# Two of six weight pieces per expert issued by ScalarE in place of SyncE, and the order of TensorE's work on expert 30, in a streamed 32-expert layer

## The reference

```python
def moe_ffn(h, w_router, b_router, w1, b1, w2, b2):
    logits = (t @ w_router + b_router)
    top_val, top_idx = lax.top_k(logits, TOP_K)          # TOP_K = 4 of 32
    gate = jax.nn.softmax(top_val, axis=-1)
    ...
    def expert_block(args):
        xb, e = args
        hid = xb @ w1[e] + b1[e]                         # w1[e]: 1024 x 2048, 8 MB
        glu, lin = jnp.split(hid, 2, axis=-1)
        glu = jnp.minimum(glu, SWIGLU_LIMIT)
        lin = jnp.clip(lin, -SWIGLU_LIMIT, SWIGLU_LIMIT)
        act = glu * jax.nn.sigmoid(SWIGLU_ALPHA * glu) * (lin + 1)
        return act @ w2[e] + b2[e]                       # w2[e]: 1024 x 1024, 4 MB
    ...
    out = jax.ops.segment_sum(ys * buf_gate[:, None], buf_tok, num_segments=n)
```

## Time and profile before

| | |
|---|---|
| median of 3 runs | 1232.0 us (1230.29 to 1233.63) |
| profiled execution, time | 1232.9 us |
| profiled execution, span from first to last instruction | 1231.1 us |
| TensorE busy | 1170.0 us, 95% |
| VectorE, ScalarE busy | 396.7 us (32%), 224.4 us (18%) |
| DMA read from HBM | 457.87 MB, 373 GB/s over the span |
| pieces of 2 MB issued by SyncE | 129 + 42 + 21 = 192 |
| wring, blk, vz pieces, issue to landing (median) | 35.6, 35.1, 35.7 us |
| granted TensorE clock, mean | 0.994 |

### The profile page before, as it was taken

How to read it: one execution, slowest core, us unless ns; L and a number is a source line. 1 busy time by engine, 2 the same in 40 slices (tenths; PEclk the granted TensorE clock), 3 DMA queues, 4 the chain that set the end, 5 groups by cost and what they waited for, 6 DMA issues and landing times.

```text
span 1231.1 us, 14120 instructions
## 1 busy us (share of the span) xinstructions
PE 1170.0 (95%) x5773; PEld 586.2 (48%) x5773; DVE 396.7 (32%) x716; ACT 224.4 (18%) x338; POOL 45.1 (4%) x32
## 2 busy tenths in 40 slices
PE   9999999999999999999998989899999999899897
PEld 8988888884343443434332323334333333233336
DVE  2679944643121221222121222212121212221127
ACT  4766564350000000000000000000000000000017
POOL 6600000010000000000000000000000000000000
PEclk9999999999999999999999999999999999999899
DMA  8655488789999999999999999999999999999980
GB/s 272 201 170 205 137 296 326 275 303 400 427 431 426 426 429 426 431 427 428 430 428 427 427 432 426 429 429 425 428 430 426 428 428 428 426 429 429 425 331 35
DMA packets 62382, 459.60 MB, mean 373 GB/s; under 512 B 7385, under 2 KB 16993, under 8 KB 37506
## 3 DMA queue, kind: packets, MB, share of 16 engines
q1 hardware_dynamic: 62338, 458.95, 90.7%
HBM read 457.87 MB, written 1.06 MB: 373 GB/s over the span
## 4 chain that ended last, share of the span: by engine, by line
PE 69%; DMA 24%; DVE 4%; ACT 2%; issue 1%; ACTq 0%; SPq 0%; DVEq 0%
PE bank L1028 23%; PE bank L1066 14%; DMA wring<-in_w_dram 12%; DMA vz<-in_w_dram 12%; PE bank L710 5%; PE bank L712 5%; PE bank L711 5%; PE bank L991 4%; PE bank L1000 2%; PE bank L1034 2%; PE bank L1057 1%; PE bank L775 1%; PE bank L785 1%; PE bank L780 1%; PE bank L697 1%
## 5 line engine op out<-in xcount | busy, mean ns | idle before, releaser
L1028 PE MATMUL bank<-wring,hT 128*64 128x512 f32 x1360 | 312.4, 603 | 17.0 <-DMA wring<-in_w_dram 13.4
L1028 PEld LDWEIGHTS bank<-wring,hT 128*64 128x64 f32 x1360 | 94.7, 138 | 201.3 <-issue 172.7
L1066 PE MATMUL bank<-wring,xbcT 128*64 128x512 f32 x672 | 150.7, 595 | 7.3 <-DVE xbcT L1998 6.3
L1979 DVE TENSOR_SCALAR xbcT<-bank 128x512 f32<-128x512 f32 x32 | 22.2, 693 | 412.7 <-PE bank L1034 412.7
L1488 ACT ACTIVATE xbcT<-xbcT 128x512 f32<-128x512 f32 x32 | 20.2, 631 | 495.2 <-DVE xbcT L1979 495.2
L2000 DVE COPY xbcT<-bank 128x256 f32<-128x256 f32 x32 | 13.6, 425 | 253.5 <-PE bank L1007 253.5
L1066 PEld LDWEIGHTS bank<-wring,xbcT 128*64 128x64 f32 x672 | 46.5, 137 | 101.4 <-issue 91.9
L1626 DVE TENSOR_TENSOR blk_lo<-blk,blk_hi 128x2048 fp32r<-128x2048 f32 x32 | 73.1, 2288 | 39.8 <-ACT blk_hi L1303 39.8
L1028 PE MATMUL bank<-vz,hT 128*64 128x512 f32 x336 | 78.9, 600 | 5.5 <-DMA vz<-in_w_dram 5.5
L1493 ACT ACTIVATE xbcT<-bank 128x512 f32<-128x512 f32 x31 | 18.5, 597 | 352.3 <-PE bank L1066 352.3
L1028 PE MATMUL bank<-blk,hT 128*64 128x512 f32 x352 | 79.7, 594 | 1.8 <-DMA blk<-in_w_dram 1.8
(11 more groups left out here) (300 smaller groups left out, 1213.6 us busy)
## 6 DMA issues: line engine op xcount, KB each, us to landing
wring<-in_w_dram SPq DMA_DIRECT2D x129, 2048.0 KB, 35.6
blk<-in_w_dram SPq DMA_DIRECT2D x42, 2048.0 KB, 35.1
vz<-in_w_dram SPq DMA_DIRECT2D x21, 2048.0 KB, 35.7
blk<-in_w_in_dram SPq DMA_DIRECT2D x28, 1024.0 KB, 5.2
blk<-in_w_branch_a_dram SPq DMA_DIRECT2D x4, 1024.0 KB, 5.5
blk<-in_w_branch_b_dram SPq DMA_DIRECT2D x4, 1024.0 KB, 7.2
blk<-in_w_out_dram SPq DMA_DIRECT2D x4, 1024.0 KB, 5.2
x<-in_x_dram SPq DMA_DIRECT2D x4, 512.0 KB, 5.3
```

Of the source, the lines that this page charges most:

```text
L1028: last = mm(bank[dh * SLOTS:(dh + 1) * SLOTS, :], xgT[:, k, :], at(c)[:, kk * 2 * F + off + dh * W:kk * 2 * F + off + (dh + 1) * W], start ...
L1066: last = mm(YB[dh * SLOTS:(dh + 1) * SLOTS, :], units[:, kk * P + c * SLOTS:kk * P + (c + 1) * SLOTS], at(W1C + c)[:, kk * D + dh * W:kk * ...
L1979: ts(g_sb, GLU[:, :], LIMIT, None, ALU.min).then_inc(g_done, 1)
```

## The change

`ACT_LOADS = (1, 2)`: from expert 2 on, pieces 1 and 2 of an expert's six are issued by ScalarE, both behind its `take_y` of the expert two before; in the list of the last twelve these are positions 1 and 2 of each six: (30, 1), (30, 2), (31, 3) and (30, 4). SyncE issues the other four, with the waits that it had. The gate weights of the embedding wait on SyncE until the last but one of the 192 pieces has landed.

On TensorE, an odd expert's gate rows are transposed into GLU ahead of `turned_units`, in place of into TB behind `rows_out`; an even expert first waits until VectorE has copied them. Expert 30 takes its four w1 pieces one after another, then gathers for expert 31, turns its units, and scatters expert 29's rows.

```diff
+ACT_LOADS = (1, 2)
@@ SyncE, in the loop
                     for c in range(NCH):
-                        g = NCH * (2 + r) + c
-                        slot = g % NSLOT
-                        sp.wait_ge(chunk_used, NCH * GROUP * i + (g - NSLOT + 1))
-                        sp.dma_start(slots[slot], chunk_src(GROUP * i + (2 + r), c)).then_inc(loaded[slot], 16)
+                        if c not in ACT_LOADS:
+                            g = NCH * (2 + r) + c
+                            slot = g % NSLOT
+                            sp.wait_ge(chunk_used, NCH * GROUP * i + (g - NSLOT + 1))
+                            sp.dma_start(slots[slot], chunk_src(GROUP * i + (2 + r), c)).then_inc(loaded[slot], 16)
@@ SyncE, after the loop
+            last_but_one = NCH * E - 2
             sp.wait_ge(chunk_used, NCH * E - NSLOT + 1)
+            sp.wait_ge(loaded[last_but_one % NSLOT], 16 * (last_but_one // NSLOT + 1))
             load_gate(0, 0)
@@ TensorE, units_of
+                if side == 0 and not alone:
+                    pe.wait_ge(selT_done, j)
@@ TensorE, expert
                 if side:
+                    pe.wait_ge(g_done, j + 1)
+                    selected(GLU)
                     turned_units(j)
...
                 rows_out(actT, at, arrived)
-                selected(TB)
+                if side == 0:
+                    selected(TB)
@@ TensorE, last_two
-                units_of(first, *stream(first), 0, between=rows_between)
+                units_of(first, *stream(first), 0)
+                gather(last_chosen)
+                pe.wait_ge(selT_done, first)
                 turned_units(first)
+                scatter(lambda: None)
@@ ScalarE
+            def freed_by_rows(j, r):
+                for c in ACT_LOADS:
+                    g = NCH * (r + 2) + c
+                    act.dma_start(slots[g % NSLOT], chunk_src(j + 2, c)).then_inc(loaded[g % NSLOT], 16)
+            with act.Fori(0, LOOPED // GROUP) as i:
+                for r in range(GROUP):
+                    gated(GROUP * i + r)
+                    take_y(GROUP * i + r)
+                    freed_by_rows(GROUP * i + r, r)
```

More of the change, by code:

```diff
@@ L490, in bcast, with chunk_src @@
             return ap.to_broadcast(shape)
+        def chunk_src(e, c):
+            if c < W1C:
+                r = c * RW1 * P
+                return w1[0, e, r:r + RW1 * P, :].rearrange("(p k) n -> p (k n)", k=RW1)
+            r = (c - W1C) * RW2 * P
+            return w2[0, e, r:r + RW2 * P, :].rearrange("(p k) n -> p (k n)", k=RW2)
         block = ctx.enter_context(nc.Block())
@@ L537, in _ @@
             load(ln_b, vec(sgu_ln_b), ln_loaded)
[L539 to L545, removed]
             def load_chunk(g):
@@ L610, in _ @@
                     for c in range(NCH):
-                        g = NCH * (2 + r) + c
-                        slot = g % NSLOT
-                        sp.wait_ge(chunk_used, NCH * GROUP * i + (g - NSLOT + 1))
-                        sp.dma_start(slots[slot], chunk_src(GROUP * i + (2 + r), c)).then_inc(loaded[slot], 16)
-            for g in range(NCH * (E - GROUP), NCH * E):
[L617 to L621, removed]
+                        if c not in ACT_LOADS:
[3 more added lines that the diff above has]
+                            sp.dma_start(slots[slot], chunk_src(GROUP * i + (2 + r), c)).then_inc(loaded[slot], 16)
+            for g in range(NCH * (E - GROUP), NCH * E):
+                if g % NCH not in ACT_LOADS:
+                    sp.wait_ge(chunk_used, g - NSLOT + 1)
+                    e, c = (g // NCH, g % NCH) if g < NCH * (E - 2) else LAST_TWO[g - NCH * (E - 2)]
+                    load(slots[g % NSLOT], chunk_src(e, c), loaded[g % NSLOT])
+            last_but_one = NCH * E - 2
             sp.wait_ge(chunk_used, NCH * E - NSLOT + 1)
+            sp.wait_ge(loaded[last_but_one % NSLOT], 16 * (last_but_one // NSLOT + 1))
             load_gate(0, 0)
@@ L1129, in stream, with last_chosen @@
                     return at, arrived
[L1131 to L1138, removed]
-                units_of(first, *stream(first), 0, between=rows_between)
+                def last_chosen():
+                    pe.wait_ge(sel_done, first + 2)
+                    pe.wait_ge(y_copied, first)
+                units_of(first, *stream(first), 0)
+                gather(last_chosen)
+                pe.wait_ge(selT_done, first)
                 turned_units(first)
+                scatter(lambda: None)
                 pe.wait_ge(actT_done, first + 1)
@@ L1501, in gate_high @@
                     fn(pg_hi[b][:, k * W:(k + 1) * W], gate_raw(b, k), ACT.Copy, scale=gain).then_inc(pg_high, 1)
[L1503 to L1506, removed]
+            def freed_by_rows(j, r):
[7 more added lines that the diff above has]
+                    freed_by_rows(GROUP * i + r, r)
+            for j in range(LOOPED, E - 2):
                 gated(j)
@@ L1512, in _ @@
                 take_y(j)
+                if j < E - 4:
+                    freed_by_rows(j, j)
+                else:
+                    for c in ACT_LOADS:
+                        g = NCH * (j + 2) + c
+                        e, piece = LAST_TWO[g - NCH * (E - 2)]
+                        act.dma_start(slots[g % NSLOT], chunk_src(e, piece)).then_inc(loaded[g % NSLOT], 16)
             gated(E - 2)
@@ L1966, in _, with expert @@
             cp(n_extra[:], cnt[:, 0:1]).then_inc(extra_done, 1)
-            def expert(j, ahead=0, last_one=False):
+            def expert(j, ahead=0, odd=False, last_one=False):
                 if ahead:
@@ L1999, in expert @@
                 dve.wait_ge(selT_filled, j + 1)
-                cp(selgT.rearrange("p t s -> p (t s)"), (GLU if last_one else TB)[:, 0:TT * P]).then_inc(selT_done, 1)
+                cp(selgT.rearrange("p t s -> p (t s)"), (GLU if odd or last_one else TB)[:, 0:TT * P]).then_inc(selT_done, 1)
             with dve.Fori(0, E // 2 - 1) as i:
                 expert(2 * i, ahead=2)
-                expert(2 * i + 1)
+                expert(2 * i + 1, odd=True)
             expert(E - 2, ahead=1)
```

## The result

The changed kernel takes 1238.58 us (median of 7 runs, 1236.13 to 1239.49) against 1232.0 for the kernel before (7 runs); the ratio is 1.0048, interval 1.0037 to 1.0060. It is **slower**, by 4.6 to 7.4 us. Its profiled execution took 1238.6 us, with a span 5.7 us over that of the earlier trace rows.

What follows compares the result with a forecast made beforehand. DMA was taken to bound the kernel up to the 30th expert, at 4.89 us a piece, then TensorE. +11.3 (3 dry, 9.8 order, less 1.5 slack) - 5.8 = +5.5 us gave 1237.5, range 1226 to 1252.

Steps and rivals of the forecast that it cites:

- the hole: At expert 0's rows, about 303 to 306 us: DMA engines run dry until ScalarE issues; +3 us (2 to 4).
- Part 1: ScalarE's later issue of pieces 1 and 2: free in steady state, +3 us once, at the first expert.
- Part 2: Second ring takes turns, ScalarE's pieces pass SyncE's queue; at the end piece 180 begins 11.3 us later, dry time included.
- In mid-kernel this only moves TensorE's waits: Before the end, the changed landing order costs nothing, as DMA stays busy.
- The list of waits: TensorE would wait before the first and fourth pieces of an expert, and not before the second and third.
- Part 3: TensorE's work from the start of piece 180 to the last rows out: 48.3 us in place of 54.1, -5.8.
- the clock's 2.1: Around expert 31's start: 2.1 us gained because the granted clock would not fall, with the gather filling the 2.58 us idle.
- The rest is small: Early selT_done wait, odd experts' earlier transposes and later gate weights: no cost; gate weights covered by 9 us.
- A: Rival, no passing: ScalarE's DMAs share the ring or are served by age; -0.7, 1231.3 us; chance 13%.
- B: Rival, two rings carry more: 433 GB/s against 428, -10 us, 1227.5 with part 1; chance 17%.
- C: Rival, taking turns costs: 0.45 us a packet adds 430 us, once a piece +54 (1291), or nothing; chance 15%.

Runs made afterwards that it cites:

- the small edits undone: Changed kernel without the gate weights' wait and the early wait for selT_done, odd experts' gate rows in TB behind rows out: 1238.66 us, ratio 1.0052.

## Why the prediction was right

It said 1237.5; 1238.6 was measured. The case that it forecast is the one that came, and its steps can be set beside the trace:

| step | predicted | measured |
|---|---|---|
| data flow again after the hole | 306.7 | 307.5 |
| transfers lost | 3 | 2.9 |
| pieces to come when 180 lands | 9 | 9.0 |
| 180 begun | 1145.5 | 1145.80 |
| expert 31 begun | 1167.2 | 1166.94 |
| wait for its third piece | 0.7 | 1.06 |
| clock, 1160 to 1170 | 1.00 | 1.00 |
| last rows out begun | 1193.8 | 1193.91 |
| span | +5.5 | +5.7 |

The close match is in part luck. Piece 12 landed at 305.38 before and at 306.24 after, ahead of everything that the change moves: 0.9 of the 5.7 us between the spans, and of the moments in the table, is the chance of these two executions (over all kernels here that piece landed from 304.0 to 307.9). And by the medians the loads cost 11.1 us, where the prediction had 11.3, but the new order gave back 4.5, where it had 5.8; so the measured +6.6 is 1.1 above the +5.5.

**Part 1** held in size. ScalarE issues its first DMA 0.16 us after its copy starts, not 0.5, and in this execution the copy stood 1.07 us later than in the earlier trace rows; the first packet follows its issue by 1.04 us, as the prediction took it. The end of the hole is therefore 0.8 us later than predicted, but the pieces ahead of it are too (piece 12 by 0.9 us), so its length stays.

**Part 2** was the step with the least under it, one packet of another kind at 810, and it held. (The trace of before has 19 such packets of q8 between 320 and 1170, not one.) When both queues have pieces, each queue's land 9.79 us apart: in the changed kernel 181 at 1129.76 and 182 at 1139.54, 178 at 1133.34 between them. By the Trainium skill (DMA: Bandwidth & Descriptors, "Queues, rings and completion order") a DMA engine goes round the queues that have work, a packet at a time; these landings agree with even turns that are shorter than a piece (whole pieces in turn would land 4.89 us apart, not 3.6 and 6.2), but don't show that a turn is one packet. What was wrong is the sentence "In mid-kernel this only moves TensorE's waits". It is true of the time of the transfers, but it drew the line at expert 30. Passing at expert 29 costs too, when nothing later covers it: 1.8 to 1.9 us by the traces, in a difference of 2.4 by the medians; in the changed kernel the larger passing behind it does. The list of waits was too short as well: besides those before first and fourth pieces there are some before pieces 4 and 5, up to 3.1 us. By engine line and releaser (us in total, times, longest):

```profile
PE bank L1033 <- DMA wring<-in_w_dram: 13.4, 12, 1.3
...
PE bank L1071 <- DMA wring<-in_w_dram: 8.4, 6, 1.8
...
PE bank L1071 <- DMA blk<-in_w_dram: 6.8, 3, 3.1
```

**Part 3** came out at -6.0 (48.1 in place of 54.1) for -5.8, but not all of that is the order. With the same loads and TensorE's old order the stretch takes 52.7 us, so the new order is worth 4.6 in the traces (4.5 by the medians). The other 1.4 us come from the clock of the execution before: it was low for longer there, so that expert 30's turn and expert 31's first piece took 1.11 and 5.75 us, against 0.66 and 4.87 (granted 0.50 from 1158 to 1164 before; 0.64 and 0.51 from 1170 to 1174 in the other). The term that the prediction sized too high is thus the clock's 2.1. The same order on the old loads gives only 4.3, since there TensorE waits for the pieces that it no longer spaces out with other work. That the clock wouldn't fall was right. The reason given, that the idle time of 2.58 us is filled, isn't enough: in the kernel whose gather was moved by half there are only 0.85 and 0.79 us idle, and the clock is still at 0.50 behind them.

**The rest is small** held: no difference with the small edits undone.

**The rivals.** A, no passing, falls with the issue-to-landing times of the two queues (19.2 and 37.8 us). B, a higher rate, and C, a cost at each turn, fall together with 427 GB/s at a share of 1.01 from 1000 to 1150. Between 320 and 1170 a 16 KB packet of q1 took 0.615 us and one of q10 0.616; in the kernel with q1 alone, 0.615. C's 0.45 us belongs to the packets of q8, which do take 1.07 us in the mean with one data queue and with two, and not to the turn. B's 433 GB/s was ten microseconds of a rate that scatters about 428. The Trainium skill says (same page, "Issuing engines are not separate DMA queues") that more issuers save only issuing time; on the rate the trace agrees (427 with two, 428 with one).

The sum, from the one-queue kernel up: -4.3 for TensorE's order, +7.1 for the passing in the last two experts, +2.1 to 4.3 for the hole (+3.0 by the landings): +4.9 to 7.1, against +6.6 measured. The change puts one gain and two losses together, and the gain alone was to be had.

## What to carry to other kernels

A second issuing queue doesn't bring more bytes, it changes their order: what is issued late overtakes what is queued, and what is queued comes at half the rate. At the end of a stream, where the consumer must have the pieces in its own order, count the pieces still to come when the first one of the last stretch lands; each that was let past costs up to a piece's time (here 4.89 us). Before a load is handed to another engine, look where its queue is nearly dry, and whether that engine reaches the issue as early there. Where the transfers set the pace, work that needs no piece can lie in the waits between the pieces instead of behind them; here that took the waits for pieces 182 and 183 from 1.24 us each to none and 0.62, for a gain of 0.6 us by the traces.

## What the runs showed that I had not expected

- **Two queues take even turns at no cost.** 9.79 us a piece on each, 0.615 and 0.616 us a packet, and 878.5 to 879.1 us from piece 12 to 191 in every kernel without the hole, whether 0, 4, 54 or 58 pieces went by the second queue; 881.8 to 882.0 in every one with it.
- **A DMA is issued while its engine is busy.** ScalarE's first issue stands 0.16 us after the start of a copy of 0.60 us.
- **The granted clock fell after short idle times.** To 0.50 behind 0.85 and 0.79 us, with the gather ahead of them and four transposes between; with one of 0.78 us, and half of the gather, the scatter and the transposes ahead, it stayed at 1.00. What of this decides wasn't tried.
